# Head norms in a two-layer decoder trunk: sums of squares in four groups of 32 output rows, roots spread from four groups of 32 partitions

## The reference, cut to what matters

```python
q = partial_rope(rms_norm(z[..., c3:c4].reshape(bsz, t, ATT_HEADS, ATT_HEAD_DIM), p['att_q_norm']), pos)
k = partial_rope(rms_norm(z[..., c4:c5].reshape(bsz, t, ATT_HEADS, ATT_HEAD_DIM), p['att_k_norm']), pos)
...
q = rms_norm((h @ p['w_cq']).reshape(bsz, t, MEM_HEADS, MEM_HEAD_DIM), p['cq_norm'])
```

## Time and profile before

| | us |
|---|---|
| median of three runs | 1561.97 (1558.62 to 1564.07) |
| the profiled execution, its own time | 1565.14 |
| its span | 1563.6 |
| PE busy | 1470.0 |
| DVE busy | 973.2 |
| ACT busy | 594.1 |
| TensorE clock granted, mean over the span | 0.972 |

### The profile page before, as it was taken

One profiled execution on the slowest core, in us unless ns is written; L12 is line 12 of the kernel. 1 busy time (PEld: TensorE's weight loads), 2 busy tenths in 40 slices (PEclk: granted clock), 3 DMA queues, 4 the chain that ended last, 5 costly groups with the idle time before them and its releaser, 6 DMA issues. The chain is left out here.

```text
span 1563.6 us, 30270 instructions
## 1 busy us (share of the span) xinstructions
PE 1470.0 (94%) x11110; PEld 1386.0 (89%) x11110; DVE 973.2 (62%) x1366; ACT 594.1 (38%) x827; POOL 125.6 (8%) x167
## 2 busy tenths in 40 slices
PE   5999999968999999999989999997899998999998
PEld 4999999746978799999989999995688787999997
DVE  4766546886745467665466664578756554766643
ACT  4333344233534244333353333441445332433331
POOL 3000000342001110000000000006220110000000
PEclk7999999989999999999999999998999999999999
DMA  7566455326548647655456655552474666555552
GB/s 225 163 168 167 156 173 162 108 89 223 178 149 285 243 133 207 165 161 166 132 146 171 166 162 165 159 162 68 151 247 136 221 213 236 141 166 166 170 163 91
DMA packets 310010, 263.95 MB, mean 169 GB/s; under 512 B 7096, under 2 KB 292024, under 8 KB 309882
## 3 DMA queue, kind: packets, MB, share of 16 engines
q1 hardware_dynamic: 290242, 203.14, 43.3%
q0 software_dynamic: 13776, 48.97, 8.8%
q10 hardware_dynamic: 5896, 10.54, 2.2%
HBM read 254.65 MB, written 8.56 MB: 168 GB/s over the span
## 5 line engine op out<-in xcount | busy, mean ns | idle before, releaser
L1330 PE MATMUL pairs<-h_hi,w_hi 128*128 128x288 f32 x1824 | 545.5, 299 | 14.8 <-DVE h_lo L863 10.6
L1330 PE MATMUL pairs<-h_hi,w_lo 128*128 128x288 f32 x1824 | 544.2, 298 | 0.0
L1330 PE MATMUL pairs<-h_lo,w_hi 128*128 128x288 f32 x1824 | 543.9, 298 | 0.0
L860 DVE TENSOR_TENSOR w_lo<-raw_weights,w_hi 128x1024 fp32r<-128x1024 f32 (+1 forms) x388 | 450.3, 1202 | 135.9 <-ACT w_hi L637 132.8
L637 ACT ACTIVATE w_hi<-raw_weights 128x1024 fp32r<-128x1024 f32 (+1 forms) x388 | 382.0, 1033 | 282.6 <-PE pairs L1330 272.1
L1330 PEld LDWEIGHTS pairs<-h_hi,w_hi 128*128 128x128 f32 x1824 | 346.9, 190 | 20.0 <-DVE h_lo L863 11.2
L1330 PEld LDWEIGHTS pairs<-h_lo,w_hi 128*128 128x128 f32 x1824 | 347.7, 191 | 0.4
L1330 PEld LDWEIGHTS pairs<-h_hi,w_lo 128*128 128x128 f32 x1824 | 346.3, 190 | 0.0
L1330 PE MATMUL pairs<-g_hi,w_lo 128*128 128x288 f32 x704 | 208.7, 297 | 0.0
L1330 PE MATMUL pairs<-g_lo,w_hi 128*128 128x288 f32 x704 | 208.5, 296 | 0.0
L1330 PE MATMUL pairs<-g_hi,w_hi 128*128 128x288 f32 x704 | 207.4, 295 | 0.0
(11 more groups left out here) (266 smaller groups left out, 1527.3 us busy)
## 6 DMA issues: line engine op xcount, KB each, us to landing
raw_weights<-in_w_ffn_in SPq DMA_DIRECT2D x176, 512.0 KB
raw_weights<-in_w_ffn_out SPq DMA_DIRECT2D x32, 1024.0 KB
raw_weights<-in_w_in SPq DMA_DIRECT2D x18, 1024.0 KB
mem_kv<-in_cache_mem_k POOLq DMA_DIRECT2D x16, 1024.0 KB, 5.5
raw_weights<-in_w_ckv SPq DMA_DIRECT2D x16, 1024.0 KB
raw_weights<-in_w_ffn_out SPq DMA_DIRECT2D x16, 768.0 KB
raw_weights<-in_w_out SPq DMA_DIRECT2D x8, 1024.0 KB
raw_weights<-in_w_cq SPq DMA_DIRECT2D x8, 1024.0 KB
```

What stands on the lines that cost most here:

```text
L860: return dve.tensor_tensor(out, in0, in1, op)
L1330: return pe.matmul(out, lhsT, rhs, start=start, stop=stop, **kw)
```

## The change

The sums of the eight blocks go to four groups of 32 PSUM rows, block k of `qk_stat` to group k % 4 and row k // 4 in it, head hd of `cq_stat` to group hd and row 0. `into_row` is now 128 by 32. Matmuls that follow one another write different groups, and each group has an accumulation of its own. Root and reciprocal work on 128 partitions (most rows of a group hold zero sums). `from_row` and the roots now lie on 32 partitions of group g. `cq_stat` has one wait for all eight blocks of squares in place of four.

```diff
-for _name, _n in (("ident", P), ("causal", P), ("own", TS), ("pick", 2 * KD - 1), ...
+for _name, _n in (("ident", P), ("causal", P), ("own", TS), ("pick", 33), ...
...
-    pick = np.zeros((P, 2 * KD - 1), np.float32)
-    pick[:, KD - 1] = 1.0
+    pick = np.zeros((P, 33), np.float32)
+    pick[:, 1] = 1.0
...
-        def into_row(h):
-            at_h = COLS["pick"][0] + KD - 1 - h
-            return const[:, at_h:at_h + KD]
-        def from_row(h):
-            return ap(const, COLS["ident"][0] + h, [[0, P]], KD)
+        def into_row(e):
+            at_e = COLS["pick"][0] + 1 - e
+            return const[:, at_e:at_e + 32]
+        def quadrant(g):
+            return slice(32 * g, 32 * g + 32)
+        def from_row(g, e):
+            return ap(const, COLS["ident"][0] + 32 * g + e, [[0, P]], 32, 32 * g)
...
-                        act.activation(qk_rms[0:KD, :], G[0:KD, t % 2, 0, 0:T], ACT.Sqrt, bias=small[0:KD, 0:1], scale=1.0 / DH).then_inc(rq_ready, 1)
+                        act.activation(qk_rms[:, :], G[:, t % 2, 0, 0:T], ACT.Sqrt, bias=eps, scale=1.0 / DH).then_inc(rq_ready, 1)
...
-                        act.activation(cq_rms[0:KD, :], G[0:KD, t % 2, 0, 0:T], ACT.Sqrt, bias=small[0:KD, 0:1], scale=1.0 / MDH).then_inc(rq_ready, 1)
+                        act.activation(cq_rms[:, :], G[:, t % 2, 0, 0:T], ACT.Sqrt, bias=eps, scale=1.0 / MDH).then_inc(rq_ready, 1)
...
-                dve.reciprocal(qk_rms[0:KD, :], qk_rms[0:KD, :]).then_inc(r_ready, 1)
+                dve.reciprocal(qk_rms[:, :], qk_rms[:, :]).then_inc(r_ready, 1)
...
-                        dve.reciprocal(cq_rms[0:KD, :], cq_rms[0:KD, :]).then_inc(r_ready, 1)
+                        dve.reciprocal(cq_rms[:, :], cq_rms[:, :]).then_inc(r_ready, 1)
...
-                    ins = mm(pair[0:KD, 0, 0:T], into_row(k), qk_squares[:, k, :], k == 0, k == KD - 1)
+                    ins = mm(pair[quadrant(k % 4), 0, 0:T], into_row(k // 4), qk_squares[:, k, :], k < 4, k >= 4)
...
-                        ins = mm(pair[:, e, 0:T], from_row(2 * j + e), qk_rms[0:KD, :])
+                        hd = 2 * j + e
+                        ins = mm(pair[:, e, 0:T], from_row(hd % 4, hd // 4), qk_rms[quadrant(hd % 4), :])
...
-                        for k in range(KD):
-                            if k % 2 == 0:
-                                pe.wait_ge(zsq_ready, L * 8 + 4 + k // 2 + 1)
-                            ins = mm(pair[0:KD, 0, 0:T], into_row(k // 2), squares[:, k, :], k == 0, k == KD - 1)
+                        pe.wait_ge(zsq_ready, L * 8 + 8)
+                        for d in range(2):
+                            for hd in range(HEADS):
+                                ins = mm(pair[quadrant(hd), 0, 0:T], into_row(0), squares[:, 2 * hd + d, :], d == 0, d == 1)
...
-                                    ins = mm(pair[:, e, 0:T], from_row(2 * j + e), cq_rms[0:KD, :])
+                                    hd = 2 * j + e
+                                    ins = mm(pair[:, e, 0:T], from_row(hd, 0), cq_rms[quadrant(hd), :])
```

More of the change, by code:

```diff
@@ L56 @@
 _at = 0
-for _name, _n in (("ident", P), ("causal", P), ("own", TS), ("pick", 2 * KD - 1), ("inv_win", 2), ("inv_first", 2 * max(WINDOWS)), ("cos", T), ("sin", T), ("swap", ROPE_DIM)):
+for _name, _n in (("ident", P), ("causal", P), ("own", TS), ("pick", 33), ("inv_win", 2), ("inv_first", 2 * max(WINDOWS)), ("cos", T), ("sin", T), ("swap", ROPE_DIM)):
     COLS[_name] = (_at, _at + _n)
```

## The result

The changed kernel takes **1548.9 us** (median of five, 1545.36 to 1550.71), the kernel before 1562.36 us beside it (five, 1558.62 to 1564.34): ratio 0.991, 95% interval 0.9888 to 0.9933. The profiled execution took 1548.9 us, its span 1547.3 us at a mean clock of 0.974, against 1563.6 at 0.972.

The account below looks back on a forecast made before the run. PE, busy 94% of the span, bounds the kernel, with head norms in stretches where it waits; 5.7 + 1.3 + 0.4 = 7.4 us off the median 1561.97 gives 1554.6 us, range 1550 to 1560.5.

Parts of the forecast that it names:

- cq_stat, forecast -2.86 us a layer: Cross attention: sums shrink from 4.05 to 1.14 us, everything behind the reciprocal moves 2.86 us earlier; -5.7 us over two layers.
- Four passes at once: Sums in cq_stat: 16 passes run as four rounds, as in one sample's scores (1.07 us), taking 1.14 us.
- The first branch of e9's expectation: In cq_stat, same-group neighbours wait for each other: 13 rounds, 3.3 us for 16 passes against 1.18.
- qk_stat, -0.65 a layer: Mixer: six blocks finish early, the last two take two rounds, win(6) starts 0.65 us earlier; -1.3 us over two layers.
- The spread roots: Mixer and cross attention: a turn's two matmuls in two row groups may overlap; ends 0 and 0.76 us, taken as -0.4.
- The clock, counted as 0: Granted clock around the norms: low stretches may shift or vanish; counted 0, with 3.5 us each way for the range.
- The clock helps: Rival: a low-clock part vanishes in one or both layers, 1549 to 1552 us; chance 0.10, inside the forecast's 0.74.
- Part arrives: Rival: behind the shift, transfers or low clock on dense work give back 3 to 5 us, 1558 to 1560; chance 0.20.
- groups do not overlap: Rival: passes in different groups take turns, 1568.4 us, or go in series at the old pace, 1562; chance 0.03.
- clock turns against it: Rival: PE enters ckv(1) and win(7) at 1.2 GHz, a low stretch at each of four places, 1568.6 us; chance 0.03.
- nor does the constant's load at the start, 18 columns wider: Kernel start, cq_stat term: loading the wider constant table costs nothing.
- terms from 5.7 to 8.5: Range of the forecast: its terms together gain 5.7 to 8.5 us, with the clock 3.5 us either way.

Follow-up runs that it names:

- e3: The changed kernel with shape_consts moved to the end of memory and a hole of its old size left, so other buffers lie as before; 1557.95 us, ratio 0.9951.
- e9: The changed kernel with a head's two blocks in cq_stat one after the other, so neighbouring matmuls write the same group; 1555.99 us (one time).
- e2: The kernel before with 64 idle bytes behind shape_consts, so later buffers lie where the changed kernel has them; 1559.71 us, ratio 0.9952.
- e1: The kernel before, unchanged, run again for a second trace; 1567.68 us (one time).

## Why the prediction was right and wrong

**cq_stat, forecast -2.86 us a layer: right.** Sums and first transposes together shrink by 2.82 us, in the changed kernel and in e3. The late input was the copy of `mk`, as worked out, though by 0.02 us and not by a tenth. "Four passes at once" came from one row and held. The Trainium skill's rule in "TensorE: Matmul & The Clock Gate", Part 3 (the mechanism), would have left 1.1 us a layer; the trace disagrees, since 16 passes with their loads take 1.18 us and 12 loads 0.63 us. The first branch of e9's expectation fell as well: neighbours in different groups are not needed.

**qk_stat, -0.65 a layer: right** (0.63).

**The spread roots, -0.4: right as to mechanism, its size a matter of the clock.** `cq_root` of layer 0 lost 0.52 us. The forecast had it that the second turn is late only at half clock, and so it is: on eight rows 2.28 us and a wait of DVE, in row groups 1.33 us (e3) and none. But how much there is to save depends on where the low clock falls: e2, still on eight rows, had the full clock at that turn in layer 0 and lost the 0.52 too, while e1 (3.52 and 3.77) has 0.27 us to save in layer 0 and 0.52 in layer 1. So the 0.52 of this pair of traces is near the 0.4 partly by luck. The rule that the forecast took from the Trainium skill, "TensorEngine Tiling (Array Packing)", Restrictions and Gotchas, asks for a bank for each row tile. Here two heads in two banks do overlap (0.75 us a turn); what happens in one bank no run shows.

**The clock, counted as 0: right as far as it can be told.** From the first root turn to `win(8)` the mixer took 44.25 and 38.62 us in the two layers before, and 43.24 and 40.18 after: one layer won 1.0 us, the other lost 1.6. Of the 16.3 us between the spans 1.0 is left when norms, roots and the steps of the dense passes are taken off. "The clock helps" named nearly the right time, 1549 to 1552, by the wrong mechanism. "Part arrives", "groups do not overlap" and "clock turns against it" did not happen.

**The step that failed: "nor does the constant's load at the start, 18 columns wider".** I looked at 18 columns as bytes to load and costed them at nothing. They are also 64 bytes of address for every buffer behind, and the sum had no term for the dense products, 9120 passes and by their steps 1205 us of the span. Measured: 6.6 us by medians (e2: 0.9952, 0.9936 to 0.9967), and 7.9 us by the steps of the passes. Where the bounds of the range said "terms from 5.7 to 8.5", an unknown in 1205 us was missing. Why the address matters stays open. The trace of before could not have given its size, only the sentence that the pace of its dense passes is one value, 133.35 ns, whose cause was not known.

## What to carry to other kernels

Before costing a change, list the addresses that it moves as well as the instructions: a table that grows by some columns moves every buffer behind it, and where PE is at its pace for most of the span half a per cent can hang on that. Tell such an effect from the meant one with two kernels, the old code at the new places and the new code at the old places. When sums over partitions need few output rows, four groups of 32 columns can make them faster, here 3.4 times (4.05 to 1.18 us); whether that helps is decided by what arrives last behind them.

## What was unexpected of the hardware

- The step of fp32r passes of 128 by 288 changes with the place of the moving operand modulo 128 bytes: 133.35 ns at 32, 132.5 at 96, 132.8 at 0, and at 64 either 132.2 or 132.8, from one block of products to the next. With 256 columns it changes with the place of the weights: 118.8, 117.3 and 119.2 ns at 32, 96 and 0, and 114.0 at 64. The cause is open.
- 16 passes of 128 by 32 over four groups of rows start four at a time, whether neighbours in the stream write the same group or another (1.20 and 1.18 us).
- At half clock, two spreads in two row groups take 1.33 us where two from eight rows take 2.28; at full clock it is 0.75 and 1.23.
- Roots spread from 8 or 32 partitions were each time followed by a stretch partly at 1.2 GHz, the same spread from 128 partitions never (three traces), with about the same busy time of PE in that window (12.58 and 12.25 of 16 us). No difference in time could be shown.
